# A multiplier of one taken from SBUF instead of the instruction, and three residual additions moved from VectorE to POOL

## The reference, cut to what matters

```
u = rmsnorm(h, g_pre_mix); proj = u @ w_in            # two attentions on proj
h = h + rmsnorm(mix @ w_o, g_post_mix)                # residual 1
v = rmsnorm(h, g_pre_mlp); a = relu(v @ w_up)
h = h + rmsnorm((a*a) @ w_down, g_post_mlp)           # residual 2
gate = sigmoid(h @ w_ple_gate + b); ple = p @ w_ple_proj
h = h + rmsnorm(gate * ple, g_post_ple)               # residual 3
```

## Time and profile before

| | us |
|---|---|
| median of 3 executions | 2934.09 |
| lowest and highest | 2927.09, 2937.89 |
| the profiled execution, time | 2937.56 |
| the profiled execution, span of its instructions | 2935.7 |
| mean granted TensorE clock, share of full speed | 0.948 |

### The profile page before, as it was taken

How to read it: one execution, slowest core, us unless ns; L and a number is a source line. 1 busy time by engine, 2 the same in 40 slices (tenths; PEclk the granted TensorE clock), 3 DMA queues, 4 the chain that set the end, 5 groups by cost and what they waited for, 6 DMA issues and landing times.

```text
span 2935.7 us, 43494 instructions
## 1 busy us (share of the span) xinstructions
PE 2773.1 (94%) x16616; PEld 2400.3 (82%) x16616; DVE 1339.5 (46%) x2027; ACT 953.1 (32%) x1514; POOL 916.0 (31%) x396
## 2 busy tenths in 40 slices
PE   7999889999869999999999999989998999999999
PEld 5666668888659999888999999989997777888887
DVE  4443352223357786434352322469675434533222
ACT  3333432223332332434232322332323433333222
POOL 2110234444214322111344433434221113444444
PEclk9998879999879999988999999999999989999999
DMA  4211122222212211101222222222111101222223
GB/s 143 61 54 42 50 76 94 93 93 94 71 42 94 80 51 44 52 31 37 68 91 87 94 87 81 93 78 94 51 51 47 42 29 58 94 94 93 94 97 110
DMA packets 61809, 215.35 MB, mean 73 GB/s; under 512 B 8144, under 2 KB 8144, under 8 KB 61648
## 3 DMA queue, kind: packets, MB, share of 16 engines
q1 hardware_dynamic: 56192, 198.80, 20.7%
q10 hardware_dynamic: 5024, 12.82, 1.4%
q0 software_dynamic: 432, 1.43, 0.2%
HBM read 210.85 MB, written 2.16 MB: 73 GB/s over the span
## 4 chain that ended last, share of the span: by engine, by line
PE 55%; issue 24%; POOLq 12%; DVE 5%; ACT 2%; DVEq 2%; ACTq 0%; DMA 0%; SPq 0%; POOL 0%
PE ps L569 15%; PE ps L570 15%; PE ps L571 15%; POOLq L511 11%; PE ps L659 2%; PE ps L672 2%; PE ps L641 1%; PE ps L935 1%; ACT wh L1073 1%; PE ps L552 1%; PE ps L910 1%; DVE arena L1886 1%; PE ps L780 1%; DVE H L1582 1%; DVE arena L1579 1%
## 5 line engine op out<-in xcount | busy, mean ns | idle before, releaser
L510 POOL TENSOR_TENSOR wl<-stage,wh 128x1024 fp32r<-128x1024 f32 x374 | 907.1, 2425 | 1950.2 <-ACT wh L1073 1949.7
L569 PE MATMUL ps<-Uh,wh 128*128 128x264 f32 (+1 forms) x2768 | 945.8, 342 | 32.1 <-DVE Ul L1585 15.8
L570 PE MATMUL ps<-Ul,wh 128*128 128x264 f32 (+1 forms) x2768 | 909.8, 329 | 0.0
L571 PE MATMUL ps<-Uh,wl 128*128 128x264 f32 (+1 forms) x2768 | 907.7, 328 | 2.2 <-issue 2.2
L1073 ACT ACTIVATE wh<-stage 128x1024 fp32r<-128x1024 f32 x374 | 396.8, 1061 | 1489.7 <-PE ps L571 1487.2
L569 PEld LDWEIGHTS ps<-Uh,wh 128*128 128x128 f32 x2768 | 534.7, 193 | 122.3 <-issue 54.6
L571 PEld LDWEIGHTS ps<-Uh,wl 128*128 128x128 f32 x2768 | 533.4, 193 | 43.3
L570 PEld LDWEIGHTS ps<-Ul,wh 128*128 128x128 f32 x2768 | 535.7, 194 | 39.0 <-issue 1.9
L570 PE MATMUL ps<-HIDl,wh 128*128 128x512 f32 (+1 forms) x1024 | 347.5, 339 | 0.0
L571 PE MATMUL ps<-HIDh,wl 128*128 128x512 f32 (+1 forms) x1024 | 346.3, 338 | 0.0
L569 PE MATMUL ps<-HIDh,wh 128*128 128x512 f32 (+1 forms) x1024 | 346.2, 338 | 0.0
(11 more groups left out here) (292 smaller groups left out, 3323.3 us busy)
## 6 DMA issues: line engine op xcount, KB each, us to landing
stage<-w SPq DMA_DIRECT2D x374, 512.0 KB, 3.3
arena<-bias_rows ACTq DMA_DIRECT2D x16, 448.0 KB, 5.0
arena<-w_mla ACTq DMA_DIRECT2D x8, 384.0 KB, 3.1
H<-xT SPq DMA_DIRECT2D x8, 256.0 KB, 6.6
out<-H ACTq DMA_DIRECT2D x8, 256.0 KB, 2.8
arena<-pT SPq DMA_DIRECT2D x1, 512.0 KB, 8.1
arena<-pairs POOLq DMA_DIRECT2D x1, 512.0 KB, 4.1
arena<-causal POOLq DMA_DIRECT2D x1, 320.0 KB, 3.3
```

Source lines behind the costliest of these rows:

```text
L510: pool.tensor_tensor(wl[:, j, :], stage[:, j, :], wh[:, j, :].bitcast(F32), ALU.subtract).then_inc(w_split, 1)
L569: pe.matmul(dst, w_lead, tok.part(a_lead, h), start=(k == 0), stop=False)
L570: pe.matmul(dst, w_lead, tok.part(a_rest, h), start=False, stop=False)
L571: mm = pe.matmul(dst, w_rest, tok.part(a_lead, h), start=False, stop=(k == len(acts) - 1))
```

## The change

The three helpers of VectorE take their multiplier from a column of `ones`, a tensor of 1.0 in SBUF, instead of the number in the instruction. VectorE waits once at its start until POOL has written `ones`. In `normalized` VectorE only multiplies `M[:, k]` by gain and inverse and counts up a new semaphore `normed`. The addition to `H[:, k]` is done by POOL in a new function `residual`, which waits for `normed` tile by tile and counts up `h_ready` itself. POOL calls it three times, at the three residuals of the first block. The drain between the multiplication and the addition on VectorE is gone.

```diff
+            def residual():
+
+                for k in range(KD):
+                    pool.wait_ge(normed, n.next(normed))
+                    pool.tensor_tensor(T1.of(H[:, k, :]), T1.of(H[:, k, :]), T1.of(M[:, k, :]), ALU.add).then_inc(h_ready, 1)
+                pool.drain()
+
             rest_of_weights(ATT_UNITS + KD + AHEAD)
 
-            pool.wait_ge(h_ready, KD)
+            residual()
             pool.memset(M[:, :, META:], 0.0).then_inc(m_zero, 1)
...
-            rest_of_weights(16 * FF_GROUPS + KD + 2)
+            rest_of_weights(16 * FF_GROUPS)
+            residual()
+            rest_of_weights(KD + 2)
+            residual()
...
             def times(dst, a, b):
-                return dve.scalar_tensor_tensor(dst, a, 1.0, b, ALU.mult, ALU.mult)
+                return dve.scalar_tensor_tensor(dst, a, ones[:, 0:1], b, ALU.mult, ALU.mult)
 
             def plus(dst, a, b):
-                return dve.scalar_tensor_tensor(dst, a, 1.0, b, ALU.mult, ALU.add)
+                return dve.scalar_tensor_tensor(dst, a, ones[:, 0:1], b, ALU.mult, ALU.add)
 
             def less(dst, a, b):
-                return dve.scalar_tensor_tensor(dst, a, 1.0, b, ALU.mult, ALU.subtract)
+                return dve.scalar_tensor_tensor(dst, a, ones[:, 0:1], b, ALU.mult, ALU.subtract)
...
                 for k in range(KD):
-                    dve.scalar_tensor_tensor(tok.of(M[:, k, :]), tok.of(M[:, k, :]), col(gain, k), inverse, ALU.mult, ALU.mult)
-                    dve.drain()
-                    plus(tok.of(H[:, k, :]), tok.of(H[:, k, :]), tok.of(M[:, k, :])).then_inc(h_ready, 1)
+                    dve.scalar_tensor_tensor(tok.of(M[:, k, :]), tok.of(M[:, k, :]), col(gain, k), inverse, ALU.mult, ALU.mult).then_inc(normed, 1)
                     yield k
 
+            dve.wait_ge(consts, 1)
```

More of the change, by code:

```diff
@@ L344, in program @@
         h_ready = sem("h_ready")
+        normed = sem("normed")
         m_ready = sem("m_ready")
```

## The result

| | before | after |
|---|---|---|
| median, us | 2933.04 (6 executions) | 2953.36 (6 executions) |
| lowest and highest | 2927.09, 2939.18 | 2950.35, 2959.85 |
| the profiled execution, time | 2937.56 | 2950.91 |
| span, mean granted clock | 2935.7, 0.948 | 2949.1, 0.953 |

The ratio is 1.0077, with a 95% interval of 1.0057 to 1.0097: the change costs 20 us by the medians. The forecast was 2952 us.

The account below looks back on a forecast made before the run. TensorE, busy 94%, bounds the kernel; its waits for VectorE count. Heads 7, residuals 8.8, norms 1.5 and other instructions 1.0 make +18.3 us on 2937.56, as a median 2952; own range 2941 to 2966, whole range 2924 to 2972.

Parts of the forecast that it names:

- Total and sign: Whole kernel: slower by 18.3 us on the profiled execution, 2952 us as a median; chance of measurably slower 0.49.
- The forecast's case: Whole kernel: VectorE and POOL still block each other, terms sum to +18.3 us; chance 0.60, own range 2941 to 2966.
- POOL's addition is short: Residuals: 1.25 us per 512-column addition, bounds 1.2 and 2.4; rival of 2.0 us gives 2970, chance 0.09.
- the scalar has its effect: Helpers: the scalar is really read from SBUF; rival that it compiles back to a number gives 2943, chance 0.03.
- Cost of one scalar: Every `times`, `plus` and `less` on VectorE: +0.06 us whatever its width, between +0.05 and +0.07.
- The lock: VectorE's two-input instructions with SBUF scalar and POOL block each other, nothing saved; rival without it: -32 us, 2902, chance 0.15.
- The heads: Eight heads of the recurrence: 0.9 us each from slower helpers, between 0.2 and 1.5; 7 us in all, bounds 2 and 12.
- a small shift can push one more instruction behind POOL: In a head of the recurrence: one more VectorE instruction may wait for POOL, +0.7 us and more.
- the bound of 12: Upper bound in us on the growth of all eight heads of the recurrence, where 7 was forecast.
- The residuals: Three residual stages of the first block with additions on POOL: 3.7 + 2.7 + 2.4 = +8.8 us, range 4 to 13.
- Norms: Three norms, eight tiles each with one `less` while TensorE waits: 3 x 8 x 0.06 = 1.5 us.

Follow-up runs that it names:

- E1: Kernel before with only the scalar of the three helpers read from `ones` in SBUF, residuals left on VectorE: 2953.74 us, ratio 1.0070.
- E3: Kernel before with the scalar from SBUF in `times` alone, the recurrence's products: 2945.40 us, ratio 1.0044.
- E2: Changed kernel with the number 1.0 back in the helpers, so only the residual additions are on POOL: 2932.89 us, ratio 1.0004 to the kernel before.
- E9: Kernel before with two further VectorE operations of 0.51 us each ahead of the first head of each layer: 2927.08 us, ratio 0.9981.
- E7: Kernel before with POOL's subtraction split into two halves and the scalar from SBUF in all three helpers: 2936.61 us, ratio 1.0009.

## Why the prediction was right, step by step

**Total and sign: right.** 2952 predicted, 2953.36 measured. The forecast's case is the one that happened: the lock holds, POOL's addition is short, the scalar has its effect. The sum came out closer than its terms, as shown below.

**Cost of one scalar: right.** +0.06 us at 256 to 528 columns, as taken from 686 and 749 ns.

**The lock: right.** The `less` of the feed-forward loops stayed at 1733 ns. What the Trainium skill says under "SBUF — State Buffer", § Who interferes with whom, of a VectorE instruction with two SBUF inputs holds for one with a scalar from SBUF too, on both sides: it waits for POOL (1733 ns) and holds POOL up (1.71 us instead of 1.24).

**The heads: mechanism right as far as it goes, but one part of it is missing.** The prediction had 7 us, of 0.9 a head, and put what goes beyond 23 x 0.06 down to "a small shift can push one more instruction behind POOL". That is what happens, but not evenly: the first head of a layer grows by 6.5 to 11 us, and the second gets 1.6 to 2.2 us shorter. In the pair of profiled executions the heads did grow by 7.7 us, and TensorE's waits there by 6.7. That agreement is luck of the clock: the heads of the kernel before had 49.9 us at half clock and those of the changed kernel 34.1. By the estimate at full clock the heads grow by 15.9 us, by 14.3 with the scalar alone (E1) and by 15.1 with the scalar in the products alone (E3), above the bound of 12; against E2, whose heads also use the number but had one chance collision, it is 9 to 11. The step that the prediction lacks is the clock. It counted TensorE's waits at their length and put nothing for what TensorE's clock does after them, some 5 us in the first head of E3. It also allowed one more whole wait in a head, where the first head of E3 takes three in place of the 0.7 us felt before. By the times alone the term is not refuted: the scalar in the products costs 13 us, between 7 and 19.

**The residuals: too dear.** Predicted +8.8 us. VectorE's stages grew by 2.7 + 1.0 + 1.5 = 5.2 us, and the part alone costs 1 us, between -6 and +8 (E2; by the medians 6). At residual 1 a tile takes 3.17 us instead of 3.40, since the sum of squares is already issued when POOL ends at 386.03 (384.32 + 1.71) and needs 0.63 us from there to the next multiplication at 386.66, where 0.83 was added. At residual 2 two tiles take 4.24 us, 2.12 each instead of 2.25; at residual 3 a tile takes 2.2 instead of 2.4. POOL's timeline at residual 2, for the pace:

```profile
772.05 2.95 POOL L518 TENSOR_TENSOR H<-H,M 128x512 f32<-128x512 f32 x2 [1.28 <-DVE M L1698]
776.29 2.94 POOL L518 TENSOR_TENSOR H<-H,M 128x512 f32<-128x512 f32 x2 [1.29 <-DVE M L1698]
```

**Norms: right.** Predicted 1.5 us; VectorE's part of each of the three norms is about 0.4 us longer in E1, 1.2 in all.

So two terms were off in opposite directions, and the sum came out well partly by luck: scalar 20 (to within 8) and residuals 1 (to within 7) stand in place of what the prediction split as about 10 and 9. The experiments' parts add up to the whole within their intervals (1.0070 and 1.0004 against 1.0077).

**What stays open.** How often a chance collision like the one in E2's second layer comes up was not counted: there is one trace of each kernel. What decides whether the clock falls after a wait is not shown, nor how much of the whole price of the scalar is clock over many executions. TensorE's clock also scatters where nothing was changed: E3 reaches the first stretch of the recurrence 6.4 us earlier than the kernel before, with the same program up to there, and with 136 us at half clock instead of 157.

## What to carry to other kernels

Where two engines share a lock that is held for a whole instruction, price a slower instruction not by its own difference but by the waits it can run into, and look at how its engine's pace stands against the one that drives the other engine. Before two profiles are compared, look at how long TensorE ran at half clock in each stage: here that hid half of the loss in the heads, and made up most of the gain there of shorter pieces. Split the long instruction of the engine that idles: here two pieces gave 0.9% and four 1.0%, for 13 and 26% more busy time on an engine that had it to spare. A number in the instruction had the lower time in every pair of runs here, though with the short subtraction not beyond the interval.

## What the runs showed of the hardware that was not expected

- The same second head, with the same wait of 1.9 us, took 44.5 us where TensorE's clock fell to 0.50 for 6.8 us and 41.4 us where it stayed at 1.00 (before and E9).
- A delay of 1 us ahead of a head left that head at 39.0 us (E9), where 0.06 us on each of some 20 instructions, with the collisions that came of it, made it 49.9 (E3), of which some 5 us are clock.
- An operation that has to wait for POOL swallows the cost of its scalar entirely: 1733 ns with it, 1734 without.
- Halving the hold does not halve the price: two operations in a row met one half each and together took nearly as long as behind the whole (2.73 against 2.96 us, E7 and E3). The scalar cost 28 us there, to within 11, and 20 with the whole subtraction, to within 8.
- POOL's addition of two tensors of 512 columns takes 1.24 us, within 0.01 of what half a subtraction and the memsets' fixed part gave; its pieces of 512 and 256 columns take 1391 and 796 ns in the mean, waits for VectorE among them.
